# The exchange of halves in the second layer's rotary embedding: four DMAs of 32 rows between two buffers, in place of a permutation product on PE

## The chip, the cores and the metric

One core of one Trainium2 chip runs the whole program. The metric is the device time of one execution in microseconds, the median of three runs. PE, ACT, DVE, POOL and SP stand for TensorE, ScalarE, VectorE, GpSimd and SyncE; a DMA is issued by the sequencer of SP or of ACT, on a queue of its own.

## The reference, cut to what matters

One inference step of a decoder trunk with two layers: 1024 prompt tokens and 8 sample tokens, width 1024, all in float32. The first layer is gated linear attention, the second a dilated window attention over keys and values that all its query groups share, each beside an attention over 256 memory tokens and followed by a gated feed-forward block. Between the layers and at the start of the second, the part that the change touches is computed:

```
def rms_norm(x, g):
    y = x * rsqrt(mean(x * x, axis=-1) + EPS)
    return y * g

def rope(x, pos):                          # x (..., heads, 64)
    half = 32
    ang = pos[:, None] * theta ** (-arange(half) / half)[None, :]
    x1, x2 = x[..., :half], x[..., half:]
    return concatenate([x1 * cos(ang) - x2 * sin(ang), x2 * cos(ang) + x1 * sin(ang)], axis=-1)

# shared keys and values of the second layer
k, v = split(rms_norm(h, kv_norm) @ w_kv, 2)          # 4 heads x 64 each
k = rope(rms_norm(k, g_k), pos)
# the second layer's queries
qd, mq = split(rms_norm(h, norm1[1]) @ b_w_in, [768]) # 12 heads x 64, 4 heads x 64
qd = rope(rms_norm(qd, b_g_q), pos)
# beside it: softmax attention of mq over 256 memory tokens, then the dilated windows over k, v
```

A head has 64 features, and the rotation takes each feature together with the one 32 places further in the same head.

## The kernel before, in words

Activations are kept with features on the 128 partitions and the 1032 tokens along the row, in three chunks of 344 columns. A tile of 128 features holds two heads, so the rotation's partner of partition p is partition p ^ 32.

**The stage.** The second layer's projection has 12 weight tiles (`NB_IN`), each used for three chunks: 36 steps n, listed in `STEPS_B`. Steps 0 to 8 take the first three tiles chunk by chunk, from step 9 on a tile's three chunks follow one another. Tiles 0 and 1 are the memory queries, 2 and 3 the keys, 4 to 9 the queries, 10 and 11 the values. The 24 steps of keys and queries are rotated (`ROPE_B`: steps 2, 5 and 8 and all from 9 to 29). Every product is made of 24 matmuls, since each operand is split into a high and a low part (L961, L962, L963).

**One step on PE** (loop at L1484): the product of step n; the head sum of step n-1 (`head_sum`, L987), which adds the squares of each head and waits until DVE has normalised step n-2; the permutation product of step n-1 (L1502), which exchanges the halves of `turn_in` into PSUM bank 7; then a piece of the memory attention. That attention handles 8 blocks of tokens, one in every three steps from step 6 on: in steps 6, 9, ..., 27 the scores (L1027), two steps later the transposes (L1035), another two steps later the product with the values (L1047). Here a step with scores is called a first step, the one after it a second step, and the one with transposes a third step; a third step from 11 on is also the last step of a weight tile.

**ACT** (`kept`, L2282): when the product is done it copies it, times the gain, to `turn_in` (L2290, two buffers), then squares it (`hsq`, L1757), then makes the reciprocal root of step n-1 (L1712, L1714). In a first step the four exponentials of the attention follow (L1805).

**DVE**: the product times cosine into the result x (L3024, waits for the squares), then for step n-1: `turned` times sine (L3032), x plus `turned` (L3035), times the root (L3044, or L3041 where the result is also reordered). In a first step the maxima follow (L2477, L2480), in a second step the division (L2492). `s_rs_` counts the two instructions on `turned`.

**POOL**: when a weight tile has been used for the last time, it splits the next but two into `w_hi` (L771) and `w_lo` (L773) and scales the one after it by the norm's gain in `w_raw` (L924, `scaled`).

**SP**: loads the weight tiles, `load_unit` (L627), each waiting until POOL has split the one three before.

Of the kernel before, what the change touches and what calls it, by code (L numbers as in the profile page):

```python
# [22 lines left out]
ACT = mybir.ActivationFunctionType  # L23
# [3 lines left out]
P = 128  # L27
# [4 lines left out]
CH = T // 3  # L32
# [26 lines left out]
U_KV = U_AOUT + KT  # L59
U_BOUT = U_KV + NB_IN  # L60
NUNIT = U_BOUT + 4
# [112 lines left out]
def trunk_program(nc, x_d, mem_d, w_d, gu_d, dn_d, cst_d, lvl_d, tri_d, gain_d, gate2_d, rope_d, state_d,  # L174
# [3 lines left out]
    with ctx:  # L178
        def at(name, shape, offset, dt=F32):
            return nc.alloc_sbuf_tensor_at(name, shape, dt, offset=offset)  # L180

        def bank(i):
            return ctx.enter_context(nc.psum_tensor(f"bank{i}", [P, 512], F32))

        def sem(name):
            return ctx.enter_context(nc.semaphore(name))
# [12 lines left out]
        O_C = O_H + KT * ROW  # L199
        cst = at("cst", [P, NCST], O_C)  # L200
        ident, ones, head_ones = cst[:, 0:128], cst[:, 128:256], cst[:, 256:384]
        swap = cst[:, 384:512]
        smp_col = cst[:, 512:520]
        smp_head = cst[:, 520:776].rearrange("p (t m) -> p t m", t=2)
        gain = at("gain", [P, NG], O_C + 4128)
        mk_t = at("mk_t", [P, 2, 2, MEM], O_C + 4416)
        mv_t = at("mv_t", [P, 2, 2, MEM], O_C + 8512)
        hsq = at("hsq", [P, 2, CH], O_C + 12608)
        turn_in = at("turn_in", [P, 2, CH], O_C + 15360)
        zero = at("zero", [P, 1], O_C + 18112)  # L210
        O_L = O_C + 18144

# [120 lines left out]
        banks = [bank(i) for i in range(8)]  # L333
# [17 lines left out]
        s_ev = sem("evacuated")  # L351
# [21 lines left out]
        s_rope, s_rsw, s_rc, s_rs_ = (sem("rope_" + n) for n in ("landed", "swapped", "cos", "sin_and_sum"))  # L373
# [79 lines left out]
        ROPE_B = [i for i, (t, c) in enumerate(STEPS_B[:NB_NORM]) if t not in B_M]  # L453
# [22 lines left out]
        EV_KV = 8 + 3 * NA_IN  # L476
# [131 lines left out]
        def _(sp):  # L608
# [16 lines left out]
            def load_unit(u):  # L625
                sp.wait_ge(s_wlo, u + 1 - WSLOT)
                sp.dma_start(w_raw[:, u % WSLOT], w_d[u]).then_inc(s_w[u % WSLOT], 16)  # L627
# [127 lines left out]
                    down_load(d)  # L755

            ffn_loads(0, U_KV)
            for u in range(U_KV, NUNIT):
                if u < U_KV + WSLOT:
                    sp.wait_ge(s_dlo, DLO0 + NDOWN - (1 if u == U_KV else 0))  # L760
                load_unit(u)
            ffn_loads(1, NUNIT)

# [188 lines left out]
        def _(pe):  # L952
# [139 lines left out]
            for n, (t, c) in enumerate(STEPS_A):  # L1092
# [4 lines left out]
                if n in MEM_TURN:  # L1097

                    i = MEM_TURN.index(n)
# [5 lines left out]
                i, b = divmod(n - 3 * (A_V[0] + 1), 3)  # L1105
# [378 lines left out]
            for n, (t, c) in enumerate(STEPS_B):  # L1484
                if n < 3:
                    pe.wait_ge(s_down, ND - (3, 2, 5)[n])
                if n - 3 in ROPE_B:
                    pe.wait_ge(s_rc, ropes_before(n - 2))
                step_product(U_KV, EV_KV, NORM_KV, n, t, c)
                if n == 0:  # L1490
                    pe.wait_ge(s_down, ND - 2)
                    norm_sum(NORM_KV + 1, HK, CH)
                if n == 2:
                    norm_sum(NORM_KV + 2, HK, CH)
                if 1 <= n <= NB_NORM:
                    head_sum(HN_B + n - 1, CH)
                if n - 1 in ROPE_B:
                    i = ROPE_B.index(n - 1)
                    pe.wait_ge(s_ev, EV_KV + n)
                    if i:  # L1500
                        pe.wait_ge(s_rs_, 2 * i)
                    pe.matmul(banks[7][:, 0:CH], swap, turn_in[:, i % 2], start=True, stop=True).then_inc(s_rsw, 1)  # L1502
                mem_attention(1, mq_b, n)
                if n in SMP_PE:
                    pe.wait_ge(s_hn, rope_done(-1))
                    mem_samples(1, SMP_PE.index(n))
# [100 lines left out]
            i = 0  # L1607
            for x, (pair, g) in enumerate(MAX_ORDER):
                i = maxima_scores(i, pair, g)
# [93 lines left out]
        def _(act):  # L1703
# [164 lines left out]
            for n, (t, c) in enumerate(STEPS_A):  # L1868
                rows, scale = P, 1.0
                if t in A_Q:  # L1870
                    dst, scale = q_a[:, t - A_Q[0], chunk(c)], float(P) ** -0.5
                elif t in A_K:
                    dst = k_a[:, t - A_K[0], chunk(c)]
                elif t in A_V or t in A_G:
                    i = t - A_V[0]
# [41 lines left out]
                if t in A_G and c == NCH - 1:  # L1917
                    act.wait_ge(s_ev, 8 + 3 * (t + 1))
                    i = t - A_V[0]
# [362 lines left out]
            def kept(n):  # L2282

                t, c = STEPS_B[n]
                tile_ready(act, MM_KV, U_KV, t, c)
                if n in ROPE_B:
                    i, g = ROPE_B.index(n), HEAD_B[n][1]
                    if i >= 2:
                        act.wait_ge(s_rsw, i - 1)
                    nc.scalar.activation(turn_in[:, i % 2], banks[n % 3][:, 0:CH], ACT.Copy, scale=gain[:, g:g + 1]).then_inc(s_ev, 1)  # L2290
                    head_square(HN_B + n, banks[n % 3][:, 0:CH])
                else:
                    nc.scalar.activation(place_b(t, c), banks[n % 3][:, 0:CH], ACT.Copy).then_inc(s_ev, 1)
                    if n < NB_NORM:
                        act.wait_ge(s_ev, EV_KV + n + 1)
                        head_square(HN_B + n, HEAD_B[n][0])
# [49 lines left out]
            for i in range(12):  # L2346
                g, b = i // 4, i % 4
# [15 lines left out]
            for i in range(2 * NW):  # L2363
# [4 lines left out]
                n = len(W_STEPS[w][1])  # L2368
                for x in range(2):
                    nc.scalar.activation(pw[:, i % 2, x, 0:n], banks[2 * (i % 2) + x][:, 0:n * P].rearrange("p (n m) -> p n m", n=n), ACT.Exp,  # L2370
                                         scale=HD ** -0.5).then_inc(s_we, 1)
# [27 lines left out]
        def _(dve):  # L2399
# [106 lines left out]
            for n in range(3 * NA_IN):  # L2506
# [13 lines left out]
                if n in MEM_TURN:  # L2520
                    i = MEM_TURN.index(n)
# [5 lines left out]
                i, b = divmod(n - 3 * (A_V[0] + 1), 3)  # L2527
# [150 lines left out]
            for c in range(NCH):  # L2678
# [5 lines left out]
                if c == 1:  # L2684
                    dve.wait_ge(s_sx, SX_OUTS)
                    dve.wait_ge(s_gsmp, 48)
                    for rows, bk, g0 in ((slice(0, 4), banks[1], G_ON), (slice(4, 6), banks[2], G_ON + 1)):
                        n = rows.stop - rows.start
# [322 lines left out]
            for n in range(3 * NB_IN):  # L3011
                if n == 3:
                    wide_apply(NORM_KV + 2, 2)
                    lo_in_place(NORM_KV + 2, 2)
                if n in ROPE_B:

                    x, g, c = HEAD_B[n]
                    i = ROPE_B.index(n)
                    dve.wait_ge(s_hsq, HN_B + n + 1)
                    if i in ROPE_STAGED:  # L3020
                        j = ROPE_STAGED.index(i)
                        if j >= NSTAGE:
                            dve.wait_ge(s_hn, rope_done(ROPE_STAGED[j - NSTAGE]))
                    nc.vector.scalar_tensor_tensor(out=x, in0=banks[n % 3][:, 0:CH], scalar=gain[:, g:g + 1], in1=rope[:, 0, chunk(c)],  # L3024
                                                   op0=ALU.mult, op1=ALU.mult).then_inc(s_rc, 1)
                if n - 1 in ROPE_B:

                    x, g, c = HEAD_B[n - 1]
                    i = ROPE_B.index(n - 1)
                    turned, root = banks[7][:, 0:CH], banks[6][:, 0:CH]  # L3030
                    dve.wait_ge(s_rsw, i + 1)
                    nc.vector.tensor_tensor(turned, turned, rope[:, 1, chunk(c)], ALU.mult).then_inc(s_rs_, 1)  # L3032
                    dve.wait_ge(s_rc, i + 1)
                    dve.wait_ge(s_rs_, 2 * i + 1)
                    nc.vector.tensor_tensor(x, x, turned, ALU.add).then_inc(s_rs_, 1)  # L3035
                    dve.wait_ge(s_hrs, HN_B + n)
                    dve.wait_ge(s_rs_, 2 * i + 2)
                    if i in ROPE_STAGED:
                        t = STAGED[ROPE_STAGED.index(i)][0]
                        for into, of in turned_pieces(q_b[:, t - B_Q[0]], (t - B_Q[0]) // 2, c):  # L3040
                            op = nc.vector.tensor_tensor(into, of(x), of(root), ALU.mult)  # L3041
                        op.then_inc(s_hn, 1)
                    else:
                        nc.vector.tensor_tensor(x, x, root, ALU.mult).then_inc(s_hn, 1)  # L3044
                elif 1 <= n <= NB_NORM:
                    x, g, c = HEAD_B[n - 1]
                    head_apply(HN_B + n - 1, x, g, x)
                mem_attention(1, mq_b, n)
                if n in SMP_DVE:
                    if n == SMP_DVE[0]:  # L3050
                        dve.wait_ge(s_hn, HN_B + 8)
                    mem_samples(1, mq_b, SMP_DVE.index(n))
                if n == NB_NORM + 3:
                    dve.wait_ge(s_hn, rope_done(-1))
                    nc.vector.memset(qw_blk[:], 0.0).then_inc(s_wqb, 1)
                    dve.wait_ge(s_wqb, 1)
                    for g in range(3):
                        for t2 in range(2):
                            for par in range(2):
                                v = qw_blk[halves_of[par], g, t2]  # L3060
                                diag = bass.AP(v.tensor, v.offset + 2 * t2 + par, [[3 * 2 * NB * 32, HD], [36, NB]])
                                nc.vector.tensor_copy(diag, q_b[halves_of[par], 2 * g + t2, SEQ:T]).then_inc(s_wqb, 1)
# [48 lines left out]
            i = 0  # L3111
            for x, (pair, g) in enumerate(MAX_ORDER):
                i = maxima(i, pair, g)
# [11 lines left out]
            for g in range(3):  # L3125
                for b in range(2):
                    n = 2 * g + b
# [192 lines left out]
```

## Time and profile before

| | us |
|---|---|
| three runs: median (lowest to highest) | 2373.61 (2373.22 to 2375.04) |
| the profiled execution, its own time | 2371.33 |
| its span, from the first to the last instruction | 2369.4 |
| PE busy in the span | 2322.4 (98%) |
| DVE, ACT, POOL busy | 1213.7 (51%), 763.8 (32%), 1214.0 (51%) |
| mean granted clock of TensorE | 0.991 |

The span and the stretches are those of one profiled execution; its own time lies 2.28 us under the median of the three runs. The stage with the steps above lies between about 1290 and 1495 us of the span.

### The profile page before, as it was taken

What the parts mean: (1) busy time and instruction counts of PE and PEld (TensorE: products, weight loads), DVE (VectorE), ACT (ScalarE), POOL (GpSimd) and SP (SyncE); (2) the same over time, 40 slices, a digit from 0 to 9 for tenths busy, and PEclk for the clock granted to TensorE, in tenths of its full rate; (3) what the DMA queues carried; (4) which work ended last, traced back from release to release, by engine and by line L of the source; (5) the groups of instructions that cost most, each with busy time, mean ns of one, the idle gap of its engine ahead of it and who ended that gap; (6) DMA issues with size and microseconds to landing.
All of it is one profiled execution on the core that took longest, in us unless ns stands there. A gap on an engine that the chain in (4) does not pass through costs nothing.

```text
span 2369.4 us, 46325 instructions
## 1 busy us (share of the span) xinstructions
PE 2322.4 (98%) x17693; PEld 2222.1 (94%) x17693; DVE 1213.7 (51%) x2275; ACT 763.8 (32%) x1574; POOL 1214.0 (51%) x885
## 2 busy tenths in 40 slices
PE   7999999999999999999999999999999999999999
PEld 6899998989999999999999888778999999999999
DVE  5422105962765656545556455614765555545555
ACT  5432115341433333322223443123433333331221
POOL 5222322123387777756675431400287777765663
PEclk9999997999999999999999999999999999999999
DMA  6111122332244443445644200410324434437642
GB/s 230 48 37 36 36 81 93 113 142 76 86 135 152 138 153 126 150 195 233 242 184 149 92 28 23 171 72 18 126 99 143 152 133 151 142 138 309 242 188 90
DMA packets 102465, 305.19 MB, mean 129 GB/s; under 512 B 9632, under 2 KB 25632, under 8 KB 99760
## 3 DMA queue, kind: packets, MB, share of 16 engines
q1 hardware_dynamic: 49104, 191.52, 22.8%
q10 hardware_dynamic: 53216, 111.67, 12.6%
q8 instruction: 99, 1.62, 0.3%
q14 instruction: 46, 0.38, 0.1%
HBM read 209.80 MB, written 93.36 MB: 128 GB/s over the span
## 4 chain that ended last, share of the span: by engine, by line
PE 90%; DVE 4%; ACT 2%; issue 1%; DMA 1%; POOL 1%; ACTq 0%; DVEq 0%
PE bank L1400 11%; PE bank L1401 11%; PE bank L1402 11%; PE bank L961 8%; PE bank L963 8%; PE bank L962 8%; PE bank L1457 5%; PE bank L1459 5%; PE bank L1458 5%; PE bank L1169 2%; PE bank L1428 1%; PE bank L1427 1%; PE bank L1429 1%; PE bank L1680 1%; PE bank L1541 1%
## 5 line engine op out<-in xcount | busy, mean ns | idle before, releaser
L961 PE MATMUL bank<-x_hi,w_hi 128*128 128x344 f32 (+1 forms) x1160 | 382.1, 329 | 11.8 <-DVE x_lo L2460 5.5
L771 POOL TENSOR_TENSOR w_hi<-w_raw,zero 128x1024 fp32r<-128x1024 f32 x44 | 87.2, 1981 | 554.2 <-PE bank L963 458.1
L963 PE MATMUL bank<-x_hi,w_lo 128*128 128x344 f32 (+1 forms) x1160 | 369.6, 319 | 0.0
L962 PE MATMUL bank<-x_lo,w_hi 128*128 128x344 f32 (+1 forms) x1160 | 369.2, 318 | 0.0
L1400 PE MATMUL bank<-x_hi,f_hl 128*128 128x258 f32 x1280 | 361.8, 283 | 0.5 <-ACT hid_odd L2139 0.5
L1401 PE MATMUL bank<-x_lo,f_hl 128*128 128x258 f32 x1280 | 361.7, 283 | 0.0
L1402 PE MATMUL bank<-x_hi,f_hl 128*128 128x258 f32 x1280 | 361.1, 282 | 0.0
L1457 PE MATMUL bank<-t_in,g_hl 128*128 128x258 f32 x1008 | 285.0, 283 | 4.7 <-POOL g_hl L844 4.7
L1458 PE MATMUL bank<-t_in,g_hl 128*128 128x258 f32 x1008 | 284.4, 282 | 0.0
L1459 PE MATMUL bank<-t_in,g_hl 128*128 128x258 f32 x1008 | 284.2, 282 | 0.0
L844 POOL TENSOR_TENSOR f_hl<-f_raw,f_hl 128x512 fp32r<-128x512 f32 (+1 forms) x128 | 196.5, 1549 | 117.4 <-ACT f_hl L2079 43.8
L961 PEld LDWEIGHTS bank<-x_hi,w_hi 128*128 128x128 f32 x1160 | 219.6, 189 | 25.4 <-issue 21.7
L1400 PEld LDWEIGHTS bank<-x_hi,f_hl 128*128 128x128 f32 x1280 | 241.9, 189 | 0.9 <-issue 0.9
L1402 PEld LDWEIGHTS bank<-x_hi,f_hl 128*128 128x128 f32 x1280 | 241.7, 189 | 0.0
L1401 PEld LDWEIGHTS bank<-x_lo,f_hl 128*128 128x128 f32 x1280 | 241.6, 189 | 0.0
L962 PEld LDWEIGHTS bank<-x_lo,w_hi 128*128 128x128 f32 x1160 | 219.5, 189 | 1.7
L963 PEld LDWEIGHTS bank<-x_hi,w_lo 128*128 128x128 f32 x1160 | 219.4, 189 | 0.0
L844 POOL TENSOR_TENSOR f_hl<-f_hl_raw,f_hl 128x512 fp32r<-128x512 f32 x120 | 179.5, 1510 | 31.6 <-ACT f_hl L2120 31.6
L1457 PEld LDWEIGHTS bank<-t_in,g_hl 128*128 128x128 f32 x1008 | 190.0, 189 | 5.4 <-POOL g_hl L844 5.4
L1459 PEld LDWEIGHTS bank<-t_in,g_hl 128*128 128x128 f32 x1008 | 190.8, 189 | 0.0
L1458 PEld LDWEIGHTS bank<-t_in,g_hl 128*128 128x128 f32 x1008 | 190.4, 189 | 0.0
L1400 PE MATMUL bank<-h_r,f_hl 128*128 128x258 f32 x640 | 181.2, 283 | 0.0
(428 smaller groups left out, 5453.8 us busy)
## 6 DMA issues: line engine op xcount, KB each, us to landing
t_in<-hid_blocks SPq DMA_DIRECT2D x42, 1548.0 KB, 16.1
f_raw<-in_gu SPq DMA_DIRECT2D x88, 512.0 KB, 4.4
hid_blocks<-t_hi ACTq DMA_DIRECT2D x126, 258.0 KB, 3.6
w_raw<-in_w SPq DMA_DIRECT2D x55, 512.0 KB, 3.3
hid_blocks<-t_low ACTq DMA_DIRECT2D x72, 258.0 KB, 4.1
d_raw<-in_dn SPq DMA_DIRECT2D x24, 768.0 KB, 5.1
h<-h_ffn SPq DMA_DIRECT2D x4, 2064.0 KB, 16.3
hid_blocks<-hid_even_lo ACTq DMA_DIRECT2D x30, 258.0 KB, 5.8
```

The source lines that it names most:

```text
L771: nc.gpsimd.tensor_tensor(w_hi[:, s], w_raw[:, s], zero[:].broadcast_to([P, 1024]), ALU.add).then_inc(s_whi, 1)
L844: return nc.gpsimd.tensor_tensor(lo_, src, hi.bitcast(F32), ALU.subtract)
L961: pe.matmul(out, wh, xh, start=(i == 0), stop=False)
L962: pe.matmul(out, wh, xl, start=False, stop=False)
L963: mm = pe.matmul(out, wl, xh, start=False, stop=(i == n - 1))
L1169: mm = pe.matmul(score_bank((hh, l), 1)[:, b * HD:(b + 1) * HD].rearrange("p (n s) -> p n s", s=s), k_a[:, hh, cols], halves(q_a[:, hh, co ...
L1400: pe.matmul(out, f_hl[:, s, 0, w], xh[:, k, cols], start=(opens and k == 0), stop=False, skip_group_check=True)
L1401: pe.matmul(out, f_hl[:, s, 0, w], xl[:, k, cols], start=False, stop=False, skip_group_check=True)
L1402: mm = pe.matmul(out, f_hl[:, s, 1, w], xh[:, k, cols], start=False, stop=(k == 3), skip_group_check=True)
L1457: pe.matmul(out, g_hl[:, s, 0, w], xh, start=(opens and k == 0), stop=False, skip_group_check=True)
L1458: pe.matmul(out, g_hl[:, s, 0, w], xl, start=False, stop=False, skip_group_check=True)
L1459: mm = pe.matmul(out, g_hl[:, s, 1, w], xh, start=False, stop=(k == GT - 1), skip_group_check=True)
```

## The change

The permutation product on PE, its matrix `swap` and the use of PSUM bank 7 go. Four DMAs on SP's queue copy `turn_in` to a new buffer `turned_rows` in SBUF, 32 rows each, with the halves of each head exchanged. `turn_in` and `turned_rows` have one buffer each. SP's wait for a free `turned_rows` and ACT's wait for a free `turn_in` follow from this, and DVE reads `turned` from SBUF. Nine of the weight loads now stand between the exchanges in SP's order of work.

```
-        swap = cst[:, 384:512]
-        turn_in = at("turn_in", [P, 2, CH], O_C + 15360)
+        turn_in = at("turn_in", [P, CH], O_C + 15360)
+        turned_rows = at("turned_rows", [P, CH], O_C + 16736)
...
-            for u in range(U_KV, NUNIT):
+            for u in range(U_KV, U_KV + 6):
                 if u < U_KV + WSLOT:
                     sp.wait_ge(s_dlo, DLO0 + NDOWN - (1 if u == U_KV else 0))
                 load_unit(u)
+            KV_LOADS = (8, 9, 10, 13, 16, 19, 22, 25, 28)
+            for i, n in enumerate(ROPE_B):
+                sp.wait_ge(s_ev, EV_KV + n + 1)
+                if i:
+                    sp.wait_ge(s_rs_, 2 * i)
+                for quarter_ in range(4):
+                    to, of = 32 * quarter_, 32 * (quarter_ ^ 1)
+                    sp.dma_start(turned_rows[to:to + 32], turn_in[of:of + 32]).then_inc(s_rsw, 16)
+                if n in KV_LOADS:
+                    load_unit(U_KV + 6 + KV_LOADS.index(n))
+            for u in range(U_KV + 6 + len(KV_LOADS), NUNIT):
+                load_unit(u)
...
-                if n - 1 in ROPE_B:
-                    i = ROPE_B.index(n - 1)
-                    pe.wait_ge(s_ev, EV_KV + n)
-                    if i:
-                        pe.wait_ge(s_rs_, 2 * i)
-                    pe.matmul(banks[7][:, 0:CH], swap, turn_in[:, i % 2], start=True, stop=True).then_inc(s_rsw, 1)
...
-                    if i >= 2:
-                        act.wait_ge(s_rsw, i - 1)
-                    nc.scalar.activation(turn_in[:, i % 2], banks[n % 3][:, 0:CH], ACT.Copy, scale=gain[:, g:g + 1]).then_inc(s_ev, 1)
+                    if i >= 1:
+                        act.wait_ge(s_rsw, 64 * i)
+                    nc.scalar.activation(turn_in[:], banks[n % 3][:, 0:CH], ACT.Copy, scale=gain[:, g:g + 1]).then_inc(s_ev, 1)
...
-                    turned, root = banks[7][:, 0:CH], banks[6][:, 0:CH]
-                    dve.wait_ge(s_rsw, i + 1)
+                    turned, root = turned_rows[:], banks[6][:, 0:CH]
+                    dve.wait_ge(s_rsw, 64 * (i + 1))
```

## Rows read from the trace of the kernel before

**Rows 1.** The page's chain that ended last: shares of the span by engine.

```profile
PE 90%; DVE 4%; ACT 2%; issue 1%; DMA 1%; POOL 1%; ACTq 0%; DVEq 0%
```

**Rows 2.** Groups by line, PE, 1280 to 1480: busy us, mean ns; idle before.

```profile
L1502 PE MATMUL bank<-turn_in,cst 128*128 128x344 f32 x48 | 17.8, 452 | 0.0
```

**Rows 3.** Timeline of PE, steps 18 to 21: start us, us, engine, line.

```profile
1396.02 0.74 PE L987 MATMUL bank<-hsq,cst 128*128 128x344 f32 x2
...
1402.20 0.74 PE L987 MATMUL bank<-hsq,cst 128*128 128x344 f32 x2
...
1408.36 0.74 PE L987 MATMUL bank<-hsq,cst 128*128 128x344 f32 x2
1408.94 0.74 PE L1502 MATMUL bank<-turn_in,cst 128*128 128x344 f32 x2
1409.52 1.04 PE L1035 MATMUL bank<-cst,pr_b 128*128 128x128 f32 x8
1410.31 0.40 PE L961 MATMUL bank<-x_hi,w_hi 128*128 128x344 f32 x1
...
1414.17 0.74 PE L987 MATMUL bank<-hsq,cst 128*128 128x344 f32 x2
```

**Rows 4.** Timeline of PE, head sum of step 3, after product 4.

```profile
1316.99 0.82 PE L987 MATMUL bank<-hsq,cst 128*128 128x344 f32 x2 [0.70 <-DVE k_b L3044]
```

**Rows 5.** Timeline of DVE, step 2 normalised.

```profile
1316.33 0.51 DVE L3044 TENSOR_TENSOR k_b<-k_b,bank 128x344 f32<-128x344 f32 x1
```

**Rows 6.** Timeline without PE, steps 18 and 19.

```profile
1396.21 0.55 ACT L2290 ACTIVATE turn_in<-bank,gain 128x344 f32<-128x344 f32 x1 [2.69 <-PE bank L963]
...
1400.62 0.17 DVE L2480 TENSOR_SCALAR mem_st<-mem_st 128x4 f32<-128x4 f32 x1
1400.82 0.45 ACT L1805 ACTIVATE bank<-bank,mem_st 128x256 f32<-128x256 f32 x1 [2.89 <-DVE mem_st L2480]
...
1402.64 0.56 ACT L2290 ACTIVATE turn_in<-bank,gain 128x344 f32<-128x344 f32 x1
...
1403.57 0.58 DVE L3024 SCALAR_TENSOR_TENSOR stage<-bank,gain,rope 128x344 f32<-128x344 f32 x1 [2.79 <-ACT hsq L1757]
...
1404.07 0.51 DVE L3032 TENSOR_TENSOR bank<-bank,rope 128x344 f32<-128x344 f32 x1
1404.68 0.51 DVE L3035 TENSOR_TENSOR stage<-stage,bank 128x344 f32<-128x344 f32 x1
1405.30 0.77 DVE L3041 TENSOR_TENSOR q_b<-stage,bank 128x344 f32<-128x344 f32 x1
...
1406.19 1.29 DVE L2492 TENSOR_TENSOR pr_b<-bank,mem_st 128x512 f32<-128x512 f32 x2
```

**Rows 7.** Timeline of SP's queue: three loads issued in a row.

```profile
362.92 0.34 SPq L645 DMA_DIRECT2D ck_a<-in_cmk  x1
363.30 0.91 SPq L647 DMA_DIRECT2D cv_a<-in_cmv  x2
```

**Rows 8.** DMA issues over the span: KB each, median us from issue to landing.

```profile
out_gstate<-st ACTq DMA_DIRECT2D x4, 96.0 KB, 1.6
...
gate<-in_gate ACTq DMA_DIRECT2D x1, 32.0 KB, 2.4
```

**Rows 9.** Timeline of POOL, steps 17 and 18.

```profile
1390.54 1.90 POOL L771 TENSOR_TENSOR w_hi<-w_raw,zero 128x1024 fp32r<-128x1024 f32 x1 [11.92 <-PE bank L963]
...
1392.52 2.41 POOL L773 TENSOR_TENSOR w_lo<-w_raw,w_hi 128x1024 fp32r<-128x1024 f32 x1
...
1394.88 1.90 POOL L924 TENSOR_TENSOR w_raw<-w_raw,gain 128x1024 f32<-128x1024 f32 x1
```

**Rows 10.** Timeline of DVE in the first layer.

```profile
429.80 0.41 DVE L2579 TENSOR_TENSOR k_a<-k_a,totals 128x256 f32<-128x256 f32 x1
...
433.02 1.99 DVE L2579 TENSOR_TENSOR k_a<-k_a,totals 128x256 f32<-128x256 f32 x1 [0.42 <-PE bank L1169]
```

**Rows 11.** Timeline of POOL, same stretch.

```profile
432.39 2.35 POOL L773 TENSOR_TENSOR w_lo<-w_raw,w_hi 128x1024 fp32r<-128x1024 f32 x1
```

## The prediction

> **What bounds the kernel now.** I read the shares of the page and the chain that ended last first: PE carries 90% of the chain [rows 1], so a microsecond that PE no longer spends counts, unless PE then waits for somebody. Next the groups of PE in this stage: the permutation product runs as 48 half passes, two for each of 24 steps, with no idle time ahead of them [rows 2]. The timeline of PE gives the step. From head sum to head sum a first step (18) takes 6.18 us, a second 6.16, a third 5.81, three together 18.15 [rows 3]. In a third step the permutation product holds PE from 1408.94 to 1409.52, 0.58 us. The reader is to see there that nothing stands between the instructions: PE is the bound of the stage, not a latency.
>
> **What goes.** 24 x 0.58 = 13.9 us of PE's time. One is lost at once: in step 4 PE already waits 0.70 us at the head sum for DVE's normalising of step 2 [rows 4, 5], and DVE comes late there because of its own work for the third chunk. So step 2's product saves nothing, step 5's saves 0.58, and from step 9 on PE alone would need 18.15 - 3 x 0.58 = 16.41 us for three steps.
>
> **What comes: a loop through SP.** With one `turned_rows`, the exchange of step n starts only when DVE has added that of n-1; with one `turn_in`, ACT takes product n+1 only when the exchange of n has landed. ACT, DVE, SP and the DMA so form a loop, one turn per step:
> - ACT's copy at 1402.64 to the end of DVE's sum, 1404.68 + 0.51: 2.55 us [rows 6]. The sum's other operand is already there.
> - Waking: ACT starts 0.03 us after DVE's 1400.62 + 0.17 [rows 6]. I take 0.03 for DVE to SP and for the DMA to ACT.
> - Three issues before the fourth: 0.38, then 0.91 / 2 each, 1.29 us [rows 7].
> - The landing of the fourth, 44 KB from SBUF to SBUF. No row shows such a one. The smallest out of SBUF, 96 KB to HBM, took 1.6 us, the 32 KB from HBM into SBUF 2.4 [rows 8]. Below 1.6 could be right too, as a smaller transfer; 0 is excluded, and a gain from it as well. I take 1.6, the row that shares the source and is close in size, and keep 2.4 as the upper end.
>
> Together 2.55 + 0.03 + 1.29 + 1.6 + 0.03 = 5.50 us. Behind ACT's new wait stand the squares, DVE's cosine product and with them the bank that PE's product three steps on writes; behind SP's stand only the weight loads. In a first step ACT is held longer by the exponentials, 1396.21 to 1402.64, 6.43 us [rows 6], which contains the loop. Three steps: 6.43 + 2 x 5.50 = 17.43 us, above PE's 16.41 and still under 18.15.
>
> **What moves: the operands of DVE.** `turned` times sine and x plus `turned` had one operand in PSUM; now both of each lie in SBUF. Alone that costs nothing: with both in SBUF 256 columns took 0.41 us [rows 10], which at DVE's 0.51 for 344 is the same slope and start. But the next row of that group took 1.99 us, and POOL was in `w_lo` from 432.39 to 434.74 [rows 11]: DVE ended at 435.01, so its 0.41 us began at 434.60, 0.14 before POOL's recorded end. An instruction with two operands in SBUF waits there until POOL's is nearly over. In this stage POOL works through 1.90, 2.36 and 1.90 us back to back after each third step [rows 9], from 0.33 us after the product (1390.54; the head sum was one period before 1408.36, at 1390.21).
>
> The two instructions of DVE meet this once in three steps. In time after the third step's product: `w_hi` to 2.23, `w_lo` 2.31 to 4.72. The sine product is due at 4.36: the exchange loop lags 2.93 us behind PE there (below), and 1.43 us lie from ACT's copy to it (1404.07 - 1402.64). It waits to 4.58 and ends at 5.10. POOL's `scaled` takes its turn from 4.96 to 6.86, since 0.1 us lies between DVE's two instructions. The sum waits to 6.72 and ends at 7.23. Normalising starts 0.62 after the sum's start, at 7.34, and ends at 7.85, or at 8.11 where it reorders (0.77 us, results from step 18 on) [rows 6]. PE's head sum waits for it and starts 0.15 later, as in step 4 (1316.84 to 1316.99) [rows 4, 5]: at 8.00 or 8.26. From there a first step without the permutation, 5.60, and a second, 5.58, to the next third step's product: 19.18 or 19.44 us instead of 18.15. The lag: the sum's end 7.23, then 0.03 + 1.29 + 1.6 + 0.03, gives ACT's first step at 10.18, the third at 22.11, and PE's product ends at 19.18.
>
> The Trainium skill states this rule in "SBUF — State Buffer", section "Who interferes with whom": two SBUF inputs on VectorE contend with a GpSimd instruction that reads SBUF, and the later one blocks until the earlier has finished. The row agrees but for 0.14 us at each hand-over; by the page's wording three hand-overs cost 0.42 us more per group, 2.1 us in all, which stays inside the forecast's own range.
>
> **What costs nothing.** The nine weight loads stand later in SP's order, but a tile loaded after step 13 is used from step 27 on, and POOL's split of it waits for step 20. Each is issued behind the exchange and ahead of the next turn. POOL's own delay, some 0.4 us for DVE's sine product, has the 11.92 us in which POOL stood idle ahead of 1390.54 [rows 9]. If that cover were gone, PE would wait for `w_lo`.
>
> **The sum.** Step 5: -0.58. Steps 9 and 10, before the first collision reaches PE: -1.16. The five periods from third step 11 to 26: three of +1.03 and two of +1.29, +5.67. From step 26 on the lag is paid: 2.93 us from its product to ACT's copy, 5.6 and 6.7 for two turns, 4.9 to the end of the division on which PE's transposes in step 29 wait (1402.64 to 1406.19 + 1.29 is 4.84) [rows 6], 0.79 for these and 3.86 for product 30 [rows 3], 24.8 against the former 18.15 + 5.81 = 23.96: +0.9, less the last permutation, 0.58: +0.3. Total +4.2 us: 2375.5 for the profiled execution's 2371.33, and 2377.8 for the median of 2373.61. A measurement here tells about 0.2% (4.7 us) from no change; the forecast lies just inside.
>
> **Rivals.**
> - *The exchange lands late.* From a landing of 1.7 us on, the sine product comes behind `w_lo` and the exchange, not POOL, sets the pace. At 2.4 the loop takes 6.30 us, a third step waits another 1.2 for `scaled`, and three steps take 6.43 + 6.30 + 7.50 = 20.23 (20.49 reordered): 3 x 2.08 + 2 x 2.34 = 10.9, the edges -1.7 at the start and +1.8 at the end, where ACT lags more: +11, 2384.6. For it: four DMAs behind one another, a destination in SBUF like the 2.4 us row. Against: that row reads HBM. It makes the kernel slower beyond doubt from 1.75 on. The Trainium skill, "DMA: Bandwidth & Descriptors", section "Anatomy of one DMA — SWDGE (gpsimd) path", has a fixed 2.0 us per DMA on GpSimd's path; with its rate for 44 KB that is 2.1, and an estimate between +4.2 and +11 gives +8; no run here shows such a transfer yet.
> - *DVE does not wait for POOL here.* Then 17.43 us (17.69) hold: 3 x -0.72 + 2 x -0.46 = -3.1, the edges -1.7 and -0.6, and PE keeps 1.4 us of the lead over ACT that it builds up: -6.8, 2366.8. Against: the 1.99 us row. For: that wait is seen on a few instructions, and POOL might keep out of their way when it is itself delayed. With this and a landing of 1.1 us or less it would be PE's 16.41 and about -12.
>
> **Chances.** Forecast 0.45 (own range 2375.5 to 2380, half of it beyond 0.2%); late landing 0.33 (0.28 slower, 0.05 within); no wait 0.17 (0.15 faster, 0.02 within); something else without effect 0.05. So faster 0.15, same 0.35, slower 0.50. The range takes in the late landing with 2 us on top, 2386.5, and reaches down to 2368.5, leaving out most of the no-wait case and an extreme landing, 2 in 10.
>
> **What would show it.** The line of the permutation gone and 13.9 us of PE with it; new idle time of PE at the head sum, released by DVE's normalising, some 1.5 us in every first step; in third steps DVE's sine and sum at 1.5 to 2.3 us instead of 0.51; `scaled` longer by about 0.4; exchanges landing in about 1.6 us. Wrong would be: sine and sum at 0.51 throughout (the faster rival), more than 6 us from ACT's copy to its next in second steps, with ACT waiting for the DMA (the slower one), or PE held by `w_lo`.

## The result and the profile after

The changed kernel is slower: 2389.14 us (four runs, 2385.86 to 2390.52) against 2373.51 in the same job, a ratio of 1.0073, 95% interval 1.0061 to 1.0085. That is +15.6 us where +4.2 was forecast, and above the range's upper end of 2386.5. The profiled execution took 2390.07 us, its span 2388.2.

What was to go did go: the permutation's line is no longer there, and PE is busy 2318.8 us of the span instead of 2322.4. That is 3.6 us less and not 13.9, because some matmuls ran longer: the head sums from 1290 to 1500 us, for one, take 24.8 us (row below) and took 22.3 in the kernel before. The chain that ended last answers to [rows 1]:

```profile
PE 83%; DVE 7%; ACT 4%; DMA 3%; issue 2%; SPq 1%; POOL 1%; ACTq 0%; DVEq 0%
```

PE lost seven points of it; DVE's share rose by three, ACT's and DMA's by two each, and SP's queue has come in. The chain of waits of the same execution, cut to the stretch from 1400 to 1426 us (start, us, what), shows a turn of the loop piece by piece:

```profile
1402.34 0.55 ACT turn_in L2296
1402.88 0.36 ACT hsq L1763
1403.27 0.57 DVE q_b L3030
1403.84 0.44 DVE turned_rows L3038
...
1404.37 0.53 DVE q_b L3041
...
1404.96 0.51 SPq L769
...
1405.51 0.59 SPq L769
...
1406.15 0.59 SPq L769
...
1406.78 1.88 DMA turned_rows<-turn_in
...
1408.74 0.55 ACT turn_in L2296
...
1413.19 3.27 DMA turned_rows<-turn_in
...
1416.54 0.55 ACT turn_in L2296
...
1418.57 2.03 DVE stage L3041
...
1422.82 1.85 DMA turned_rows<-turn_in
...
1424.75 0.55 ACT turn_in L2296
```

No piece in this stretch is PE's. From copy to copy (1402.34 to 1408.74) a turn takes 6.40 us: 2.56 from the copy to the sum's end, 0.06 to SP, 1.82 from the start of the first issue to that of the fourth, 1.88 from there to its landing (its own issue included), 0.08 to ACT. PE alone would need 5.2 to 5.6 us for a step, 16.41 for three. The next two turns are longer for two different reasons: a landing of 3.27 us, then a sum that took 2.03 us instead of 0.53.

ACT's copies of steps 9 and 27 start at 1342.10 and 1471.60 us: 18 turns in 129.50 us, where the kernel before took 108.91 (1341.76 to 1450.67). Of the excess of 20.6 us, 18 turns at 6.40 make 6.3. Three turns with a late landing (1.2 to 1.5 above 6.40 each) make 4.1; six turns in which DVE waited for POOL (1.05 to 2.19 above) make 9.4; the remaining 0.8 are small pieces. The steps after 27 give some 2 us back, so that the spans of the two profiled executions differ by 18.8; the medians differ by 15.6. In 15 of the 18 turns ACT's copy starts on the landing of the exchange; in the other three (1350.69, 1437.87, 1458.71) it comes behind the exponentials of a first step.

The groups of PE by line, from 1290 to 1500 us, and three rows of the view of waits from 1280 to 1500 (engine, line, waited for: us in total, times, longest), say who waited:

```profile
L999 PE MATMUL bank<-hsq,cst 128*128 128x344 f32 x60 | 24.8, 496 | 20.0 <-DVE q_b L3047 9.6 <-DVE q_b L3050 6.6 <-DVE k_b L3050 3.8
```

```profile
ACT turn_in L2296 <- DMA turned_rows<-turn_in: 65.9, 16, 6.5
...
PE bank L999 <- DVE q_b L3047: 9.6, 9, 3.7
...
ACT turn_in L2296 <- PE bank L975: 7.5, 4, 2.9
```

In [rows 4] PE waited once, 0.70 us, at the head sum. Now it waits 20.0 us there, for DVE's normalising, and ACT's copy, which used to wait for PE, waits for the exchange. The view of the tile `turned_rows` has the exchange and the two instructions of DVE (ns minimum, median, maximum):

```profile
L769 SPq DMA_DIRECT2D turned_rows<-turn_in x96: 507/591/600, 1304.2 to 1489.2; - x96
L3038 DVE TENSOR_TENSOR turned_rows<-turned_rows,rope x24: 504/507/1730, 1315.7 to 1491.1; 128x344 f32<-128x344 f32 x24
L3041 DVE TENSOR_TENSOR stage<-stage,turned_rows x12: 517/518/2020, 1418.6 to 1491.8; 128x344 f32<-128x344 f32 x12
...
DMA to landing us min/median/max: 1.8/1.9/3.3
```

An issue took 0.59 us against 0.34 and 0.455 in [rows 7], a landing 1.9 against the 1.6 taken from [rows 8]. Last, the windows of 20 us of the same execution (busy us and count of PE, PEld, DVE, ACT, POOL; then the granted clock):

```profile
1360.00:1380.00 20.00, 14.38 (x90) 11.64 (x89) 11.32 (x24) 5.31 (x16) 6.06 (x3) 0.97 0.11 28
...
1420.00:1440.00 20.00, 18.38 (x107) 16.07 (x108) 10.20 (x22) 7.87 (x22) 4.58 (x3) 0.83 0.18 54
```

PE idles 5.6 us of the first window. There and in the next 60 us the granted clock is below 1, which it is not in any of these windows before; a part of the matmuls ran at the lower of the two levels, 1.2 GHz. In the chain from 1400 to 1426 no matmul appears, nor in the chains of the stretches around it, from 1342 to 1474 us, so the lower clock did not set the time there directly. The chain does not look inside an instruction of DVE that waits for POOL, and POOL starts when PE's product ends; a part of the clock by that way is not excluded.

### The profile page after: what moved, and what is told of

It reads as the page before. It is cut to its first block, busy times and chain, and to the rows that moved or that the text cites. A ratio compares the mean times of both kernels' runs of the same rounds, so it can differ in the third digit from the quotient of the medians.

```text
span 2388.2 us, 46326 instructions
## 1 busy us (share of the span) xinstructions
PE 2318.8 (97%) x17645; PEld 2216.5 (93%) x17645; DVE 1226.5 (51%) x2275; ACT 764.4 (32%) x1574; POOL 1218.8 (51%) x885
## 4 chain that ended last, share of the span: by engine, by line
PE 83%; DVE 7%; ACT 4%; DMA 3%; issue 2%; SPq 1%; POOL 1%; ACTq 0%; DVEq 0%
PE bank L1412 11%; PE bank L1413 11%; PE bank L1414 11%; PE bank L973 7%; PE bank L975 6%; PE bank L974 6%; PE bank L1469 5%; PE bank L1471 5%; PE bank L1470 5%; PE bank L1181 2%; DMA turned_rows<-turn_in 2%; PE bank L1440 1%; PE bank L1439 1%; SPq L769 1%; PE bank L1441 1%
## 6 DMA issues: line engine op xcount, KB each, us to landing
h<-h_ffn SPq DMA_DIRECT2D x4, 2064.0 KB, 15.6
```

## The experiments

The theory is that the exchange loop, one turn per step, sets the time, with POOL's waits and late landings inside it. The rival causes are the wait for POOL by itself and the load of 96 more transfers. The ratios are to the kernel before in the same job.

| kernel | median us | ratio (95%) |
|---|---|---|
| changed kernel | 2389.14 | 1.0073 (1.0061 to 1.0085) |
| e1 two buffers | 2363.82 | 0.9973 (0.9963 to 0.9983) |
| e2 sum from PSUM | 2382.91 | 1.0052 (1.0038 to 1.0066) |
| e3 one DMA | 2372.46 | 1.0012 (1.0002 to 1.0022) |
| e4 before, sum from SBUF | 2372.07 | 1.0004 (0.9994 to 1.0013) |
| e5 two buffers and PSUM | 2359.31 | 0.9955 (0.9940 to 0.9970) |
| e6 early release, PSUM | 2373.60 | 1.0012 (1.0002 to 1.0022) |
| e7 early release, SBUF | 2375.26 | 1.0021 (1.0011 to 1.0032) |
| e8 sine first | 2365.52 | 0.9977 (0.9968 to 0.9986) |
| e9 sine first, PSUM | 2354.19 | 0.9941 (0.9929 to 0.9954) |
| e10 as e5, again | 2356.47 | 0.9951 (0.9938 to 0.9965) |
| e11 two DMAs | 2372.93 | 1.0014 (1.0006 to 1.0023) |
| e12 six DMAs | 2415.65 | 1.0191 (1.0167 to 1.0214) |

**e1, two buffers.** It takes the loop apart and keeps all 96 transfers.

```
-                    sp.wait_ge(s_rs_, 2 * i)
+                    sp.wait_ge(s_rs_, 2 * i if i < 3 else 2 * i - 2)
...
-                    if i >= 1:
-                        act.wait_ge(s_rsw, 64 * i)
-                    nc.scalar.activation(turn_in[:], ...
+                    if i >= 2:
+                        act.wait_ge(s_rsw[i % 2], 64 * (i // 2))
+                    nc.scalar.activation(turn_in[:, i % 2], ...
```

> The changed kernel with two buffers each for turn_in and turned_rows (room made by a staging pool of 3 instead of 5 tiles), so that ACT's copy of a step waits for the exchange two steps back, and SP's issue for the sum two steps back. Theory loop (one turn of copy, products, four issues and landing took 6.40 us, and nothing else can be under way in it): the loop no longer sets the pace, PE does with its 5.6 us per step; the changed kernel's excess goes and part of the 13.9 us of removed PE time shows: 2362 to 2370 us. Rival port (DVE's wait for POOL, some 1.5 us in each group of three steps, is the loss by itself): those waits stay where they are, at most the 6.9 us of the loop's plain lengthening go, about 2380 us. Rival DMA load (96 more transfers disturb others): unchanged, 2389 us.

Measured 2363.8, as the loop theory has it: by the ratios some 24 us under the changed kernel, and 0.27% under the kernel before. The transfers are all still there, so their load is not the cause. Nor is POOL by itself, since DVE waits for it more than in the changed kernel. The groups of DVE from 1290 to 1500 us (busy us, mean ns):

```profile
L3044 DVE TENSOR_TENSOR turned_rows<-turned_rows,rope 128x344 f32<-128x344 f32 x23 | 16.4, 713 | 3.6 <-DMA turned_rows<-turn_in 3.6
L3047 DVE TENSOR_TENSOR stage<-stage,turned_rows 128x344 f32<-128x344 f32 x12 | 12.3, 1021 | 1.3
...
L3047 DVE TENSOR_TENSOR q_b<-q_b,turned_rows 128x344 f32<-128x344 f32 x6 | 7.1, 1190 | 0.6
L3047 DVE TENSOR_TENSOR k_b<-k_b,turned_rows 128x344 f32<-128x344 f32 x5 | 7.1, 1421 | 0.5
```

These make 42.9 us, with two short rows of 0.5 that are not shown 43.9. In the changed kernel the 48 instructions took 34.7 (14.8 + 7.7 + 6.1 + 6.1 in the same view), and without any wait they would take 24.6. So DVE lost 19 us to POOL here and 10 there, and this kernel is the faster one: outside the loop PE's lead pays for most of it. The timeline of one third step shows both instructions caught:

```profile
1403.59 1.89 POOL L789 TENSOR_TENSOR w_hi<-w_raw,zero 128x1024 fp32r<-128x1024 f32 x1 [10.62 <-PE bank L981]
1404.88 0.98 DVE L3044 TENSOR_TENSOR turned_rows<-turned_rows,rope 128x344 f32<-128x344 f32 x1
1405.56 2.56 POOL L791 TENSOR_TENSOR w_lo<-w_raw,w_hi 128x1024 fp32r<-128x1024 f32 x1
1405.96 2.53 DVE L3047 TENSOR_TENSOR stage<-stage,turned_rows 128x344 f32<-128x344 f32 x1
1408.08 2.16 POOL L942 TENSOR_TENSOR w_raw<-w_raw,gain 128x1024 f32<-128x1024 f32 x1
```

The sum ends at 1408.49, so its own 0.52 began at 1407.97, 0.15 before POOL's recorded end at 1408.12.

**e2, sum from PSUM.** The sine product goes to PSUM bank 7, which the change had left free, and the sum reads it there.

```
-                    nc.vector.tensor_tensor(turned, turned, rope[:, 1, chunk(c)], ALU.mult).then_inc(s_rs_, 1)
+                    summand = banks[7][:, 0:CH]
+                    nc.vector.tensor_tensor(summand, turned, rope[:, 1, chunk(c)], ALU.mult).then_inc(s_rs_, 1)
...
-                    nc.vector.tensor_tensor(x, x, turned, ALU.add).then_inc(s_rs_, 1)
+                    nc.vector.tensor_tensor(x, x, summand, ALU.add).then_inc(s_rs_, 1)
```

> The changed kernel, but DVE's sine product goes to PSUM bank 7 and the sum reads it there, so that of the two only the sine product still has both operands in SBUF. Theory loop with the port inside it: the sum's waits for POOL (2.02 us instead of 0.51, six of them) go and with them up to 9 us; the loop turn of 6.40 us stays: 2380 to 2383 us. Rival (POOL's turn then falls on the sine product instead, which now meets it): the wait moves from the one line to the other, 2387 to 2390 us. Rival port alone: 2375 us or less.

Measured 2382.9, in the theory's range by the median; by the ratio the gain is 0.2 points, 5 us, some way towards the first rival. Every sum takes 0.51 us now, and part of the wait moved to the sine product: 16.2 us for 24 of them instead of 14.8. The shortest turns are still 6.41 us.

**e3, one DMA.** One issue in place of four of 128 rows, which leaves out the exchange of halves.

```
-                for quarter_ in range(4):
-                    to, of = 32 * quarter_, 32 * (quarter_ ^ 1)
-                    sp.dma_start(turned_rows[to:to + 32], turn_in[of:of + 32]).then_inc(s_rsw, 16)
+                sp.dma_start(turned_rows[:], turn_in[:]).then_inc(s_rsw, 16)
```

> The changed kernel with one DMA of 128 rows in place of the four of 32 rows; it leaves out the exchange of halves (each row gets its own back), all else is as before. Theory loop: the three issues ahead of the fourth (1.82 us) leave every turn, 6.40 becomes about 4.6 us if one transfer of 172 KB lands as fast as one of 43 KB, below PE's 5.6; the port's waits then show only in part: 2365 to 2373 us. If the larger transfer lands later by 1 us, the turn is 5.6 us and the time about 2375. Rival port: only the plain lengthening of the loop goes, about 2380 us.

Measured 2372.5, in the theory's range. The shortest turns are 4.83 us, with a landing of 2.1 us for 172 KB. That is under PE's pace, yet the kernel is not faster than before: the first steps still take 6.4 us and more, and DVE waits for POOL in both instructions (the sine product alone 20.9 us for 24).

**e4, the kernel before with the sum's operands in SBUF.** PE keeps its permutation; only the place of the sine product changes.

```
-                    nc.vector.tensor_tensor(turned, turned, rope[:, 1, chunk(c)], ALU.mult).then_inc(s_rs_, 1)
+                    nc.vector.tensor_tensor(sine_rows[:], turned, rope[:, 1, chunk(c)], ALU.mult).then_inc(s_rs_, 1)
...
-                    nc.vector.tensor_tensor(x, x, turned, ALU.add).then_inc(s_rs_, 1)
+                    nc.vector.tensor_tensor(x, x, sine_rows[:], ALU.add).then_inc(s_rs_, 1)
```

> The kernel before with its permutation product on PE, but the sine product is written to a buffer in SBUF (staging pool of 4 instead of 5 tiles for the room), so that the sum has both operands in SBUF as in the changed kernel; no exchange, no loop. Theory loop: DVE's sum waits some 1.5 us for POOL once in three steps, yet PE works ahead and covers it: 2373 to 2376 us. Rival port: the wait reaches PE's head sum, six times 1.5 us, 2382 us. Rival no wait: the sum takes 0.51 us throughout, 2373.5 us.

No change, but the theory's wait hardly occurs, so the run says nothing on its price. Of 24 sums one took 1.63 us and nearly all others 0.52. Here the sum comes just ahead of POOL's `w_lo`, and POOL waits instead, as the timeline shows:

```profile
1392.82 0.52 DVE L3036 TENSOR_TENSOR q_b<-q_b,sine_rows 128x344 f32<-128x344 f32 x1
1392.89 2.71 POOL L774 TENSOR_TENSOR w_lo<-w_raw,w_hi 128x1024 fp32r<-128x1024 f32 x1
```

`w_lo` takes 2.71 us, where it takes 2.36 alone. Whoever is first makes the other wait.

**e5, two buffers and PSUM** (the edits of e1 and e2).

> The changed kernel with both edits: two buffers each for turn_in and turned_rows, and the sine product in PSUM bank 7 so that the sum no longer has both operands in SBUF. With two buffers alone it took 2363.8 us, with PSUM alone 2382.9. Theory (the port's wait costs only inside the loop; outside it PE's lead covers most of it): PE idles some 7 us at the head sum in the run with two buffers, about half of it behind DVE's normalising, so 2360 to 2363 us. Rival (the two effects simply add, -7 us for PSUM whatever the loop): 2357 us. Rival (the wait moves to the sine product): 2363 to 2365 us.

Measured 0.9955, 10.7 us under the kernel before; e10, the same kernel again, gave 0.9951. PE's idle time at the head sum falls from 6.9 us in e1 to 1.4. The gain over e1, 4.3 us, is that of e2 over the changed kernel, so the two edits come close to adding up, with a smaller amount than the rival's 7; the time lies just under the theory's range. What a wait of DVE costs differs all the same. In e2 the 48 instructions took 28.4 us instead of the changed kernel's 34.7: 6 us of waits gone, 5 us of time. In e5 they took 27.8 instead of e1's 43.9: 16 us of waits gone, 4 to 5 us of time.

**e6 and e7, early release.** Both keep single buffers and let SP go after the sine product instead of the sum; in e6 that product is in PSUM, in e7 in a buffer of its own in SBUF.

```
-                    sp.wait_ge(s_rs_, 2 * i)
+                    sp.wait_ge(s_rs_, 2 * i - 1 if i else 0)
```

> The changed kernel with its single buffers, the sine product in PSUM bank 7, and SP waiting for the sine product of the step before, which is then the last reader of turned_rows, instead of for the sum. Theory loop: the products of DVE leave the loop, which is left with copy (0.50), four issues (1.82 and the landing of 1.88) and two hand-overs, about 4.3 us, under PE's 5.6; so nearly the time of two buffers, 2360 to 2366 us. Rival (the wait of ACT for the landing still holds the squares and the cosine product, so that DVE's sine product of a step ends the next turn too): the turn is about 5.6 to 6.0 us and the time 2372 to 2380 us.

> The changed kernel with its single buffers, the sine product written to a buffer of its own in SBUF (staging pool of 4 instead of 5 tiles), and SP waiting for the sine product of the step before instead of for the sum. The loop is cut as in the run with PSUM, but the sum keeps both operands in SBUF and waits for POOL. Theory (port costs only what the loop passes on): the sum's wait lies outside the loop, so within 2 us of the run with PSUM, 2361 to 2368 us. Rival port alone (some 7 us whatever the loop, as between the changed kernel and its run with PSUM): 2369 to 2373 us.

The theory missed here, and e6's rival was right; e7 lies above both its ranges, though within the 2 us of e6 that its theory gave. Measured: 1.0012 and 1.0021, with shortest turns of 5.80 and 5.79. Only the sum left the loop, 0.6 us. The squares and the cosine product stay in it, because DVE's program has the cosine product of step n ahead of the sine product of n-1, and the squares of n stand behind ACT's copy, which waits for the exchange of n-1. The difference of e6 and e7, 1.7 us by the medians, is within the intervals.

**e8 and e9, sine first.** e8 is the changed kernel with that order turned round and nothing else (the cosine product's lines, unchanged, in a function of their own); e9 adds e6's PSUM and early release.

```
-                if n in ROPE_B:
...
+                if n in ROPE_B and n - 1 not in ROPE_B:
+                    cos_product(n)
                 if n - 1 in ROPE_B:
...
                     nc.vector.tensor_tensor(x, x, turned, ALU.add).then_inc(s_rs_, 1)
+                    if n in ROPE_B:
+                        cos_product(n)
```

> The changed kernel with one change of order on DVE and nothing else: the sine product and the sum of step n-1 are issued ahead of the cosine product of step n instead of behind it. Single buffers, the sum's both operands in SBUF, four issues, all as in the changed kernel. Theory: in the changed kernel the cosine product of step n holds DVE's sine product of n-1 back until ACT has copied and squared step n, which itself waited for the exchange of n-1; with the other order the turn loses the squares (0.35) and the cosine product (0.58) and ACT's copy runs beside the sine product: landing to sum end 0.03 + 0.51 + 0.10 + 0.51, then 0.04 + 1.82 + 1.88 + 0.04, about 4.9 us instead of 6.40, under PE's 5.6: 2361 to 2368 us. Rival (the port's waits of 1.5 us in the loop bring it back to PE's pace or above): 2369 to 2375 us. Rival (order does not matter, the transfers do): 2387 us or more.

> The same order, and besides the sine product in PSUM bank 7 with SP waiting for it instead of for the sum (single buffers still). Theory: the turn is then ACT's copy or the sine product (0.55), 1.82 for the issues, 1.88 for the landing and three hand-overs, about 4.4 us, and only the sine product can meet POOL: the full gain without second buffers, as in the run with two buffers and PSUM, 2357 to 2362 us. Rival (the turn is still in PE's way in some steps): 2363 to 2370 us.

> The kernel with two buffers and the sine product in PSUM once more, beside the two runs of the same call, for their order: 0.995 to 0.996 of the kernel before, about 2360 us, and within 0.1% of the run with the sine product first and in PSUM.

The order alone takes 0.96 points, some 23 us, off the changed kernel and puts it under the kernel before; with PSUM and the early release it is 0.9941, some 14 us under, about the 13.9 us of PE that were to be won and below the range expected for e9. e9 and e10 overlap in their intervals. In e9 the chain from 1400 to 1426 is PE's alone again, as the line that sums it up shows:

```profile
by line: PE bank L973 25.4%; PE bank L975 23.6%; PE bank L974 23.5%; PE bank L999 11.1%; PE bank L1039 8.2%; PE bank L1059 5.3%; PE bank L1047 3.4%
```

**e11 and e12, two and six DMAs.** The loop's length as a dose: e11 has two DMAs of 64 rows, which leaves out the exchange of halves as e3 does, e12 two of 32 rows and four of 16.

```
-                for quarter_ in range(4):
-                    to, of = 32 * quarter_, 32 * (quarter_ ^ 1)
-                    sp.dma_start(turned_rows[to:to + 32], turn_in[of:of + 32]).then_inc(s_rsw, 16)
+                for half_ in range(2):
+                    to = 64 * half_
+                    sp.dma_start(turned_rows[to:to + 64], turn_in[to:to + 64]).then_inc(s_rsw, 16)
```

> The changed kernel with two DMAs of 64 rows each in place of the four; it leaves out the exchange of halves (each row gets its own back). It puts the turn near the one of the forecast, 5.50 us: 6.40 less two issues of 0.60, plus some 0.1 for a larger landing, 5.3 us. Theory (the turn sets the time): 20 turns less 1.1 us each than the changed kernel, less where PE or a first step's exponentials take over, so 2370 to 2377 us, near the forecast of 2377.8 or under it. With one DMA the turn was 4.83 and the time 2372.5, so at least that: 2372 to 2377. Rival (transfers, not issues, are what counts): 2385 us or more.

> The changed kernel with six DMAs in place of four (two of 32 rows, four of 16 rows, the same bytes to the same places). Theory (the turn is issues plus landing and sets the time): two more issues of 0.60 us in each of some 20 turns, 20 x 1.2 = +24 us on the changed kernel, less where its late landings or POOL's waits now fall into the longer turn: 2405 to 2414 us. Rival (the changed kernel is held by POOL or the late landings, not by each turn): +10 us or less, 2390 to 2399 us.

e12 came out at 2415.7, a little over the theory's range, with its shortest turns at 7.63 us; e11 at 2372.9, within its range. The chain of waits of e12 has the turn, five issues ahead of the sixth:

```profile
1418.48 0.51 SPq L771
...
1421.58 1.84 DMA turned_rows<-turn_in
...
1423.50 0.55 ACT turn_in L2298
```

From its copy at 1415.86 that is 7.64. With 2.56 for ACT and DVE, 0.14 of hand-overs, the issues and the landing, the turn works out as 4.8 us for one DMA (2.1), 5.3 for two (0.5 and 2.1), 6.4 for four (1.82 and 1.88), 7.6 for six (3.10 and 1.84); measured 4.83, 5.33, 6.40, 7.64. Up to about PE's pace the time hardly moves (1.0012 and 1.0014; 1.0021 in e7 with 5.79 us); from there it rises steeply, and from four DMAs to six 1.24 us more in a turn cost 1.18 points, some 28 us. With one or two DMAs three steps take some 19.2 us all the same, where PE alone needs 16.4: there POOL sets the end of the sum, as the rows of e11 in the next section show, and a shorter turn only makes the sine product wait longer, 2.2 us in most groups of e3 against 1.1 in e11.

## Why the prediction was wrong, step by step

- **What goes** was right: the permutation's line and its idle-free place in PE's order are gone, and PE's pace of 16.41 us for three steps is there where nothing holds PE: in e5 and e9 four periods in a row take 16.42 or 16.43.
- **The step that failed is the size of the loop**: "Three issues before the fourth: 0.38, then 0.91 / 2 each, 1.29 us" and "The landing of the fourth ... I take 1.6". They measured 1.82 and 1.88. The rest of the sum, 2.55 and two times 0.03, measured 2.56, 0.06 and 0.08. So the turn was 6.40 instead of 5.50 us, and it went from about PE's pace, 16.41 for three steps, to well over it. DVE's two instructions no longer came where the forecast had them against POOL, and from step 9 to 27 the loop, with waits for POOL and late landings inside it, sets the time. The landing was taken from a transfer to HBM, and the issues from a pair that were loads; neither writes SBUF from SBUF.
- **The rival "the exchange lands late"** had the mechanism. It said "from a landing of 1.7 us on", and priced a turn of 6.30 at +11. The measured turn is 6.40, and that it is so close is luck: the landing took 1.88 us, not 2.4, and the issues made up for it (1.82 instead of 1.29). 0.1 us on some 20 turns make 2 more, and three landings of 3.1 to 3.3 us, which neither case had, another 4.1. That is 17, near the measured 15.6; this sum is argued and not tested by itself.
- **The sum at its own loop was right.** e11's turn of 5.33 us is close to the 5.50 of the forecast, and the instructions come where it had them:

```profile
1406.35 1.89 POOL L783 TENSOR_TENSOR w_hi<-w_raw,zero 128x1024 fp32r<-128x1024 f32 x1 [12.74 <-PE bank L975]
1409.93 1.16 DVE L3038 TENSOR_TENSOR turned_rows<-turned_rows,rope 128x344 f32<-128x344 f32 x1
1411.20 2.02 DVE L3041 TENSOR_TENSOR stage<-stage,turned_rows 128x344 f32<-128x344 f32 x1
1414.29 0.82 PE L999 MATMUL bank<-hsq,cst 128*128 128x344 f32 x2 [1.36 <-DVE q_b L3047]
```

  Counted from the start of `w_hi`, the sine product ends at 4.74 us, the sum at 6.87, and PE's head sum starts at 7.94; the forecast had 4.77, 6.90 and 7.93. (PE also waits 0.3 to 0.6 us in third steps, which the forecast did not have.) ACT's copies give the period of three steps:

```profile
1408.51 0.55 ACT L2296 ACTIVATE turn_in<-bank,gain 128x344 f32<-128x344 f32 x1 [3.61 <-DMA turned_rows<-turn_in]
1415.99 0.55 ACT L2296 ACTIVATE turn_in<-bank,gain 128x344 f32<-128x344 f32 x1 [4.76 <-DMA turned_rows<-turn_in]
1422.71 0.56 ACT L2296 ACTIVATE turn_in<-bank,gain 128x344 f32<-128x344 f32 x1
1428.05 0.55 ACT L2296 ACTIVATE turn_in<-bank,gain 128x344 f32<-128x344 f32 x1 [3.61 <-DMA turned_rows<-turn_in]
```

  1408.51 to 1428.05 is 19.54 us, and the four other periods are 19.13, 19.24, 19.27 and 19.64, against the forecast's 19.18 and 19.44. Its ratio of 1.0014 is +3.3 us, against +4.2. So it is the two terms of the loop that failed, and not the way from the loop to the time.
- **The wait for POOL** was right in kind and in its early hand-over, 0.15 us against the 0.14 of [rows 10, 11]. In the changed kernel it caught mostly one instruction of a group, not both, since the longer loop shifts DVE against POOL, as in the sum of 1418.57 above (2.03 us; POOL's `w_hi` ran from 1418.05 to 1420.22). The rival "DVE does not wait for POOL here" is refuted by those rows. The Trainium skill, "SBUF — State Buffer", section "Who interferes with whom", also says that the order of issue decides who blocks; e1 (DVE blocked) and e4 (POOL blocked) agree.
- **The landing on the page's figure**: the estimate of 2.1 us from the Trainium skill, "DMA: Bandwidth & Descriptors", section "Anatomy of one DMA — SWDGE (gpsimd) path", was nearer than the 1.6 chosen. The trace has 1.88 for 43 KB on SP's queue, a path that section is not about.
- **What costs nothing** held: the weight loads are issued behind the exchange, and no wait of PE for `w_lo` shows among the longer rows of the view of waits.
- **What was not seen**: that DVE's order, cosine product of n before sine product of n-1, puts the copy's wait in front of work whose data have landed. The prediction took the 2.55 us from copy to sum as given. e8 shows that some 1.5 us of the turn was order only: there the sum ends 1.17 us after the landing at 1380.55, in the changed kernel 2.64 us after it (0.08 and 2.56).

```profile
1380.57 0.53 DVE turned_rows L3041
1381.19 0.53 DVE q_b L3044
```

What delays three of the landings to over 3 us was not settled. The longest landing was 2.4 us in e7, 2.7 in e11 and 2.8 to 3.7 in the other nine kernels with an exchange.

## What to carry to other kernels

Where work moves from an engine to a DMA between single buffers, write down the whole loop that it closes, from the producer's next write back to itself, and compare one turn with the pace of the bound engine: here PE's pace was 5.2 to 5.6 us a step, and 0.8 us more of issue and landing than forecast put the turn well beyond it. A turn under that pace was not enough either, as long as DVE also waited for POOL: 19.2 us for three steps (e3, e11) instead of 16.4 (e9). Then look whether an instruction of the next round stands, in program order, ahead of the one that frees the buffer: turning that order round was worth about as much as a second buffer. An instruction moved from PSUM to SBUF operands can wait for POOL, but what that costs depends on whether it lies inside such a loop: some 0.8 us of time per us of waiting inside it (e2), some 0.3 outside it (e5).

## What the runs showed of the hardware

- Issues of SP that follow one another took 0.51, then 0.59 us with 0.04 between them for 32 rows, where [rows 7] had 0.34 and 0.91 for two. One DMA of 172 KB inside SBUF landed 2.1 us after the start of its issue, one of 43 KB 1.9: size hardly counted here, the number of issues did.
- In some runs whose PE waited at the head sums the granted clock of windows of 20 us fell as low as 0.83. In the changed kernel (longest wait 3.7 us) the four windows from 1360 to 1440 are below 1, in e12 (6.0 us) those from 1380 to 1500, in e7 (2.9 us) two, at 0.91 and 0.83, in e2 (4.1 us) and e3 (1.9 us) one each, at 0.92 and 0.91. In e1, e6, e8, e9 and e11, with waits of at most 1.8 us, none from 1340 to 1440 is.
- A PSUM bank that the removed product had used served to keep one of DVE's two instructions from ever waiting for POOL: all 24 sums of e2 took 0.51 us.
